# Seven elementwise products per pair of an RWKV-7 recurrence, moved from GpSimd to VectorE

## The reference

```python
kk = kk / jnp.maximum(jnp.linalg.norm(kk, axis=-1, keepdims=True), NORM_EPS)
decay = exp(-exp(w_log));  a = sigmoid(a0 + lora_a);  k_dir = k * (1.0 + (a - 1.0) * k_a)
def step(S, inp):
    r_t, w_t, k_t, v_t, kk_t, a_t = inp
    sa = jnp.einsum('bhvk,bhk->bhv', S, -kk_t)
    S = (S * w_t[:, :, None, :] + sa[..., None] * (kk_t * a_t)[:, :, None, :]
         + v_t[..., None] * k_t[:, :, None, :])
    return S, jnp.einsum('bhvk,bhk->bhv', S, r_t)
bonus = sum over directions of sum(r * k_dir * r_k) * v
```

## Time and profile before

| | |
|---|---|
| median of 3 runs | 2422.64 us (2421.42 to 2424.56) |
| the profiled execution's own time | 2427.65 us |
| its span in the profile | 2425.4 us |
| mean granted TensorE clock | 0.937 of full speed |
| busy: TensorE, VectorE, ScalarE, GpSimd | 2139.6, 1103.0, 866.2, 473.0 us |
| instructions in the span | 60962 |

### The profile page before, as it was taken

The page is one execution under the profiler, slowest core; times in us unless marked ns, Lnnn a source line. Parts: engine busy times, 40 slices in busy tenths (PEclk is TensorE's granted clock), DMA queues, the critical chain, the costliest instruction groups (busy, mean ns, idle before and its releaser), DMA issues. The chain is left out here.

```text
span 2425.4 us, 60962 instructions
## 1 busy us (share of the span) xinstructions
PE 2139.6 (88%) x26707; PEld 1755.3 (72%) x26707; DVE 1103.0 (45%) x1515; ACT 866.2 (36%) x1426; POOL 473.0 (20%) x339
## 2 busy tenths in 40 slices
PE   6799897778778887769899999999897978999998
PEld 4587685567666776658788888888874547788887
DVE  3733324566777677532422222222457534333333
ACT  2223223465556565431423112221233533431231
POOL 0312311654565546301000000001120001000000
PEclk8799998799989999989899999999898998999999
DMA  9666754001100010031122212221110012332332
GB/s 303 191 200 194 217 164 127 18 14 31 32 25 16 27 32 11 11 147 52 53 63 69 71 48 61 66 74 51 49 57 9 0 35 69 95 107 84 95 108 82
DMA packets 262162, 191.78 MB, mean 79 GB/s; under 512 B 11946, under 2 KB 252468, under 8 KB 261428
## 3 DMA queue, kind: packets, MB, share of 16 engines
q1 hardware_dynamic: 261940, 188.45, 25.7%
HBM read 170.60 MB, written 17.83 MB: 78 GB/s over the span
## 5 line engine op out<-in xcount | busy, mean ns | idle before, releaser
L520 DVE TENSOR_TENSOR ffn_lo<-ffn_raw,ffn_hi 128x1024 fp32r<-128x1024 f32 (+1 forms) x120 | 159.8, 1331 | 547.4 <-ACT ffn_hi L515 547.4
L527 PE MATMUL banks<-operand_hi,ffn_hi 128*128 128x512 f32 (+1 forms) x1056 | 377.1, 357 | 15.3 <-DVE operand_lo L486 12.2
L528 PE MATMUL banks<-operand_lo,ffn_hi 128*128 128x512 f32 (+1 forms) x1056 | 377.6, 358 | 0.0
L529 PE MATMUL banks<-operand_hi,ffn_lo 128*128 128x512 f32 (+1 forms) x1056 | 374.8, 355 | 0.0
L515 ACT CAST ffn_hi<-ffn_raw 128x1024 fp32r<-128x1024 f32 (+1 forms) x120 | 136.3, 1136 | 508.2 <-PE banks L529 507.4
L1832 POOL TENSOR_TENSOR lvl<-sc_b,level_mask 128x512 f32<-128x512 f32 x144 | 195.1, 1370 | 207.3 <-DVE sc_b L1586 132.8
L527 PEld LDWEIGHTS banks<-operand_hi,ffn_hi 128*128 128x128 f32 x1056 | 200.4, 190 | 46.7 <-DVE operand_lo L486 12.8
L529 PEld LDWEIGHTS banks<-operand_hi,ffn_lo 128*128 128x128 f32 x1056 | 199.6, 189 | 30.0
L528 PEld LDWEIGHTS banks<-operand_lo,ffn_hi 128*128 128x128 f32 x1056 | 200.2, 190 | 27.9
L528 PE MATMUL banks<-ffn_g_lo,ffn_hi 128*128 128x512 f32 (+1 forms) x528 | 188.0, 356 | 0.0
L527 PE MATMUL banks<-ffn_g_hi,ffn_hi 128*128 128x512 f32 (+1 forms) x528 | 187.4, 355 | 0.0
(11 more groups left out here) (256 smaller groups left out, 4681.8 us busy)
## 6 DMA issues: line engine op xcount, KB each, us to landing
mod_raw<-in_mod_w SPq DMA_DIRECT2D x96, 512.0 KB, 6.1
ffn_raw<-in_ff_w SPq DMA_DIRECT2D x88, 512.0 KB, 3.8
ffn_raw<-in_ff_w SPq DMA_DIRECT2D x32, 704.0 KB, 4.7
proj_raw<-in_rw_wr SPq DMA_DIRECT2D x8, 512.0 KB, 4.7
proj_raw<-in_rw_wk SPq DMA_DIRECT2D x8, 512.0 KB, 4.6
proj_raw<-in_rw_wv SPq DMA_DIRECT2D x8, 512.0 KB, 4.8
rwkv_out_raw<-in_rw_wo SPq DMA_DIRECT2D x8, 512.0 KB, 4.3
qk_w_raw<-in_at_wq SPq DMA_DIRECT2D x8, 512.0 KB, 4.0
```

Source lines behind the costliest of these rows:

```text
L520: signal(eng, eng.tensor_tensor(self.lo[s][:, 0:k_tiles, :], self.raw[s][:, 0:k_tiles, :], self.hi[s][:, 0:k_tiles, :].bitcast(F32), ALU.s ...
L527: pe.matmul(out, w[0], x[0], start=first, stop=False)
L528: pe.matmul(out, w[0], x[1], start=False, stop=False)
L529: return pe.matmul(out, w[1], x[0], start=False, stop=last)
```

## The change

The seven features are entered as VectorE's in `ENGINE`. With that, the exception for pair 0 (`LEADING`) goes, and `engine_of` has one argument less. VectorE's branch for `r_decay` takes over the waits that GpSimd's had (for the outputs and the states of the pair before last, whose buffers it writes). GpSimd's `feature` is deleted, so GpSimd keeps `cut` and `diag`. The hand-written order is as it was, so each product stands in VectorE's queue where the order names it.

```diff
@@ ENGINE, engine_of @@
-                  "b_gate0": "pool", "b_gate1": "pool", "k_gate0": "pool", "k_gate1": "pool", "k_sum": "pool",
-                  "r_decay0": "pool", "r_decay1": "pool"}
+                  "b_gate0": "dve", "b_gate1": "dve", "k_gate0": "dve", "k_gate1": "dve", "k_sum": "dve",
+                  "r_decay0": "dve", "r_decay1": "dve"}
-        LEADING = ("b_gate0", "b_gate1", "k_gate0", "k_gate1", "k_sum", "r_decay0", "r_decay1")
-        engine_of = lambda t, name: "dve" if t == 0 and name in LEADING else ENGINE[name] if name in ENGINE else READOUT[name]
+        engine_of = lambda name: ENGINE[name] if name in ENGINE else READOUT[name]
@@ VectorE, feature @@
                         elif name in ("r_decay0", "r_decay1"):
                             e = int(name[7])
                             after(dve, use, t, f"through{e}")
-                            dve.wait_ge(slices[0], 48)
+                            if t == 0:
+                                dve.wait_ge(slices[0], 48)
+                            need(dve, y_ready, NCH * (t - 1))
                             ins = v.tensor_tensor(ar[s][e][:, :, 1, :], chunks(r_s[s]), through(e), ALU.mult)
                             if e == 1:
                                 after(dve, use, t, "through0")
+                                need(dve, s_done, NCH * (t - 1))
                                 v.tensor_copy(ends[s][:, 0, :], ep[0][:, :, CH:CH + 1].rearrange("p n o -> p (n o)"))
                                 ins = v.tensor_copy(ends[s][:, 1, :], ep[1][:, :, 0:1].rearrange("p n o -> p (n o)"))
@@ GpSimd @@
-                    def feature(self, t, name):
-                        if engine_of(t, name) != "pool":
-                            return
...
-                        ins.then_inc(features["pool"], 1)
```

More of the change, by code:

```diff
@@ L920, in after @@
                 if t >= 0:
-                    eng.wait_ge(features[engine_of(t, name)], use.of(engine_of(t, name), t, name) + 1)
+                    eng.wait_ge(features[engine_of(name)], use.of(engine_of(name), t, name) + 1)
         def side(use, t, name):
@@ L1028, in feature @@
             def feature(t, name):
-                use.take(engine_of(t, name), t, name)
-                if engine_of(t, name) == "pe" and not opens(t, name):
+                use.take(engine_of(name), t, name)
+                if engine_of(name) == "pe" and not opens(t, name):
                     use.take("work", "side", t, name)
@@ L1532, in feature @@
                     def feature(self, t, name):
-                        if engine_of(t, name) != "pe":
+                        if engine_of(name) != "pe":
                             return
@@ L1621, in feature @@
                     def feature(self, t, name):
-                        if engine_of(t, name) != "dve":
+                        if engine_of(name) != "dve":
                             return
@@ L1754, in feature @@
                     def feature(self, t, name):
-                        if engine_of(t, name) != "act":
+                        if engine_of(name) != "act":
                             return
@@ L1835, in cut @@
                             .then_inc(lvl_ready, 1)
-                    def feature(self, t, name):
-                        if engine_of(t, name) != "pool":
-                            return
[L1840 to L1846, removed]
-                            after(pool, use, t, f"key_gate{e}")
-                            ins = g.tensor_tensor(k_in[s][e][:], k_in[s][e][:], k_s[s][:], ALU.mult)
-                        elif name == "k_sum":
-                            after(pool, use, t, "k_gate0", "k_gate1", "kk_sum")
-                            ins = g.tensor_tensor(tmp[:], k_in[s][0][:], k_in[s][1][:], ALU.add)
-                        elif name in ("r_decay0", "r_decay1"):
-                            e = int(name[7])
-                            after(pool, use, t, f"through{e}")
-                            need(pool, y_ready, NCH * (t - 1))
-                            ins = g.tensor_tensor(ar[s][e][:, :, 1, :], chunks(r_s[s]), through(e), ALU.mult)
-                            if e == 1:
-                                after(pool, use, t, "through0")
-                                need(pool, s_done, NCH * (t - 1))
-                                g.tensor_copy(ends[s][:, 0, :], ep[0][:, :, CH:CH + 1].rearrange("p n o -> p (n o)"))
-                                ins = g.tensor_copy(ends[s][:, 1, :], ep[1][:, :, 0:1].rearrange("p n o -> p (n o)"))
-                        ins.then_inc(features["pool"], 1)
                 pool.wait_ge(tables, 6)
```

## The result

The changed kernel takes 2454.95 us at the median of six runs (2443.89 to 2464.04); the kernel before, run beside it, 2423.60 (2418.31 to 2429.24). The ratio is 1.0116, 95% interval 1.0095 to 1.0136: slower by about 28 us by the ratio; the two medians lie 31 us apart. The profiled execution took 2451.98 us, with a span of 2450.2, which is 24.8 more than the span of 2425.4 before. The profile of before includes a delay of 4.9 us in one pair (672 to 684 us: TensorE stops once for 1.53 us, and from 674 to 684 its granted clock is 0.50) that most profiles here do not have. The forecast was +14, to 2436.6: the direction was right, the size half of it. The time lies inside the stated 2416 to 2458, near its upper end, and above the 2428 to 2450 to which the forecast gave most of its chance.

What follows compares the result with a forecast made beforehand. No engine is full: the recurrence is bound by TensorE's queue plus what it waits for. Last slots 7.1 and first slots 9.1 make 16.2 us, less 2 gives +14, a median of 2436.6; range 2416 to 2458.

Steps and rivals of the forecast that it cites:

- End of the second slot: Added products ahead of the state update behind kk make it, and TensorE's next multiplication with the state, 3.6 us late.
- the walk: The prediction's step-by-step tracing of one pair's instructions through the queues, from the end of the second slot onward.
- The mask ahead of level 3: Last slot: GpSimd's first level mask comes early, so TensorE's 1.68 us stall before 842.65 goes.
- Level 3: Last slot, first level product: 3.6 us late less 1.7 returned by the earlier mask, so 1.9 late.
- First slot: r_decay0 and masks delay a_decay0 and the transpose by 2.0 us, 0.65 returned: +1.3 a pair, 9.1 in seven.
- VectorE's room of 5.5 to 8.7 us a slot: Rival, whole recurrence: VectorE's idle time hides the additions under TensorE, no change, 2423 us; chance 0.17.
- the buy-back: Rival, whole recurrence: shorter locks and vanished stalls return 16.5 us, so the kernel gets faster, 2406 us; chance 0.13.
- the +53 of a VectorE that bounds everything: Rival, whole recurrence: 7.6 us a pair on VectorE all reaches TensorE, 2476 us; chance 0.15.
- the sum of the last slot: Last slot, delays less returns: +0.8 us in the pair walked, some +2.3 in one pair, 7.1 in seven.
- the one on the slack: Last slot: mask waits of 0.5 and 1.2 us vanish in 2.5 us of slack before a state update, costing nothing.
- the return at level 1: Last slot, before 853.79: the 1.79 us stall for a transpose goes, leaving 0.2 us late instead of 1.9.
- The 2 us taken off for stalls inside a step: Whole kernel: some of TensorE's "issue" stalls would fall into the new waits, so 16.2 us becomes +14.

Runs made afterwards that it cites:

- e1: Kernel before with only k_gate0, k_gate1 and k_sum moved to VectorE; 2443.16 us against 2425.05, ratio 1.0075.
- e2: Kernel before with only b_gate0 and b_gate1 moved to VectorE; 2426.70 us, ratio 1.0000.
- e11: Changed kernel with the first score multiplications issued four times ahead of TensorE's wait in six last slots; 2448.36 us against 2427.49, ratio 1.0088.
- e9: Changed kernel with the seven products of pair 1 back on GpSimd; 2456.38 us, ratio 1.0111 to the kernel before.

## Why the prediction was right in kind and half of the size

**Right.** *End of the second slot.* The update was to come 6.5 us after the start of kk; it comes 6.34 after (847.83 to 854.17). TensorE waits 3.28 for it. The order differs a little from the walk: the mask begins 0.08 us behind the scan, so it stands in the way of the second product (1.0 us) and not of the scan (1.27). *The mask ahead of level 3.* TensorE's stop before the first level product of the last slot is gone, 0.0 us in six of six where 0.2 to 1.8 stood before. *Level 3.* 3.6 late less 1.7 returned was to give 1.9; it is 2.65, and with TensorE's clock kept up 1.60. *First slot.* +1.3 forecast, +1.1 measured; TensorE's wait for the transpose was to be 0.42 + 2.0 and is 1.99 there and up to 2.59 elsewhere. VectorE in that place, answers to the earlier trace rows:
```profile
884.75 1.65 DVE L1680 TENSOR_TENSOR ar<-r_pair,ep 128x768 f32<-128x768 f32 x1
886.33 2.02 DVE L1662 SCALAR_TENSOR_TENSOR ar<-kk,ep 128x768 f32<-128x768 f32 x1
888.28 0.68 DVE L1597 TENSOR_TENSOR inverse<-banks,inverse 128x512 f32<-128x512 f32 x1
```
The walk had a_decay0 end at 872.7, 3.7 us behind its old start; here it ends 3.6 behind the start of r_decay0. r_decay1 shows no cost: level 3 of the first slot comes no later (-0.62). *The rivals.* VectorE's room of 5.5 to 8.7 us a slot did not hide the additions, the buy-back did not outweigh them, and the +53 of a VectorE that bounds everything did not come.

**Wrong: the sum of the last slot.** +0.8 was forecast and +3.15 measured, 2.35 x 6 = 14 us over six pairs. It comes from before level 4 (1.4), before level 3 (0.75) and before level 1 (0.4), less 0.2 in the other two.

*The step that failed is the one on the slack: the bonus product and the first b product each meet a mask (0.5 and 1.2 us), "which the 2.5 us of slack before the update of 848.88 takes up".* Level 4 was to come no later than level 3 and comes 1.38 us later. Two things are wrong in the step. The first is the slack, which was read in one pair. The addition and transpose that level 4 needs, kernel before:
```profile
844.95 0.69 DVE L1598 TENSOR_TENSOR inverse<-banks,inverse 128x512 f32<-128x512 f32 x1 [1.58 <-PE banks L1370]
845.68 0.71 DVE L1605 STREAM_TRANSPOSE inverse_t<-inverse 128x512 f32<-128x512 f32 x1
```
The transpose ends at 846.39, and TensorE starts level 4 at 848.91: 2.5 us to spare. But the same difference in all six pairs, from the traces of before and after, is
```
slot     2     5     8    11    14    17    mean
before  1.96  2.05  1.24  0.15  2.53  1.25  1.53
after   0.15  0.15  0.15  0.15  0.15  0.15  0.15
```
I had walked the pair with the most. The other five have 1.3 on average, and in the one with none (slot 11) the time before level 4 grew by 3.0 us. On the mean 1.0 us less is taken up than the walk assumed. After, the transpose is what level 4 waits for in every pair, the one walked (slot 14) included: there level 4 comes 0.5 us later.

The second is the delay. The walk set 1.7 us, two waits for masks, against the slack. By the same difference the transpose comes 2.9 us later in the pair walked, counted from the start of the level 3 product, and 2.8 on the mean of six. The masks of VectorE ahead of it show where the rest is from, kernel before and then after:
```profile
841.01 0.69 DVE L1586 TENSOR_TENSOR sc_b<-banks,score_mask 128x512 f32<-128x512 f32 x1 [0.48 <-PE banks L1317]
```
```profile
860.39 0.69 DVE L1585 TENSOR_TENSOR sc_b<-banks,score_mask 128x512 f32<-128x512 f32 x1 [1.73 <-PE banks L1316]
```
The mask stood 1.6 us ahead of the level 3 product of 842.65 and stands 0.5 behind that of 859.92. It waits for scores that TensorE makes behind the late update, and the return at level 3 does not reach it. That is 2.1 of the 2.9. The other 0.8 arises between the mask's start and the transpose's end (5.38 us, then 6.15). There the walk's terms would give 1.1: waits of 1.7, b_gate0's own 0.95, which it left out in this step, less the 1.58 us for which VectorE sat idle ahead of the addition. The single parts agree: by the table and the same slack, the transpose is 0.8 us later with the keys alone (e1) and 1.4 with the b products alone (e2). The mean slack takes up either, but not both.

*A second term was not in the sum at all:* behind a wait of 3.3 us TensorE's own work gets longer. e11, in one trace, prices it at 1.05 us a last slot. Without it the time before level 3 is 1.60, 0.3 under the forecast's 1.9. The row of the pair walked had shown a clock of 0.85, and I did not ask what had lowered it. Windows of the kernel before in that pair:
```profile
840.00:843.00 3.00, 1.32 (x53) 1.11 (x50) 2.52 (x6) 1.62 (x3) 3.00 (x5) 1.00 0.00 0
...
845.00:848.50 3.50, 2.49 (x86) 2.30 (x82) 1.35 (x2) 1.07 (x3) 3.50 (x3) 0.50 0.02 5
848.50:851.00 2.50, 2.50 (x84) 2.45 (x84) 2.12 (x4) 1.79 (x4) 2.50 (x3) 0.50 0.00 0
```
TensorE works for 1.32 us of three, and a little later it runs at 0.50. Part of the 2.5 us of slack may be made of just that; no run tests it.

*The third is the return at level 1:* I counted 1.7 us for the second stall of the earlier trace rows, and 1.32 came on the mean (by pair between 3.0 returned and 0.3 lost). Together: 1.38 before level 4 (1.0 of it the slack of the other pairs, 0.4 the delay), 1.05 less 0.3 before level 3, 0.4 at level 1, less 0.2 (the other two products, +0.44 instead of +0.6) is the 2.35.

*Smaller misses.* The 0.65 that the bonus add in the first slot was to give back did not come: it still met a mask, that of 895.94, and took 1.42 us at 896.60. GpSimd's busy time fell by 84 us and not by 90 to 110, as its masks grew by 21. The 4.5 us of the start, where the walk counted 2.1 for pair 1, come and go between traces of kernels that are equally fast (see e9); their cause stays open. The second slot's -1.2 is mostly the one delay of before. The 2 us taken off for stalls inside a step can be neither shown nor refuted beside delays of that size.

## What to carry to other kernels

Before an instruction is moved to an engine "with room", ask which consumer stands behind it in that engine's queue: three products ahead of one state update made +18 us, and all seven, with two of the three behind it and four others behind transposes, nothing that could be told. Slack that a term rests on has to be measured in every repetition and taken at its mean, not read in the one that was walked (2.53 us there, 1.53 on the mean), and all delays that meet in it have to be set against it together: two that it takes up singly (0.8 and 1.4 us) it does not take up at once. Parts that are each free can so cost something together. A wait on TensorE has two prices, its length and the clock behind it; a look at the granted clock of the stretch behind the wait tells the second. Whether buying the second price back makes the whole kernel faster is open here.

## What was not expected of the hardware

Behind an idle stretch of 3.2 us TensorE's granted clock stood at 0.50 for 5.4 us, and the six last slots took 6.57 us more of its time (98.88 against 92.31). 48 superfluous multiplications ahead of each wait kept the clock at 1.00 behind the wait and made the six slots 6.0 us shorter, though not the twenty slots together. Where VectorE and GpSimd both had work queued (861.2 to 866.3 us), they alternated one instruction at a time: a product of 0.95 us took 2.02, and three masks 5.16 us instead of 3.8.
